# Chunked RWKV-7 recurrence rearranged: compact 32-wide diagonal blocks, the inverse of one chunk issued among the state and output of the chunk before

## What is computed

```python
def rwkv7_scan(r, w, k, v, a, b):
    def step(state, inp):
        r_t, w_t, k_t, v_t, a_t, b_t = inp
        sa = jnp.einsum("bhvk,bhk->bhv", state, a_t)
        state = (state * w_t[:, :, None, :] + sa[..., None] * b_t[:, :, None, :]
                 + v_t[..., None] * k_t[:, :, None, :])
        return state, jnp.einsum("bhvk,bhk->bhv", state, r_t)
...
def squared_relu_mlp(h, w_up, w_down):
    return jnp.square(jax.nn.relu(h @ w_up)) @ w_down
```

## Time and profile before

| | us |
|---|---|
| median of 3 runs (2734.05 to 2739.23) | 2734.75 |
| profiled execution | 2739.59 |
| its span, first to last instruction | 2737.8 |
| TensorE busy in it | 2587.3 (95%) |
| VectorE, ScalarE, GpSimd busy | 1136.0, 696.1, 320.1 |
| mean granted TensorE clock | 0.979 of 2.4 GHz |

### The profile page before, as it was taken

The page is one execution under the profiler, slowest core; times in us unless marked ns, Lnnn a source line. Parts: engine busy times, 40 slices in busy tenths (PEclk is TensorE's granted clock), DMA queues, the critical chain, the costliest instruction groups (busy, mean ns, idle before and its releaser), DMA issues.

```text
span 2737.8 us, 34644 instructions
## 1 busy us (share of the span) xinstructions
PE 2587.3 (95%) x13906; PEld 2140.4 (78%) x13906; DVE 1136.0 (41%) x1331; ACT 696.1 (25%) x1053; POOL 320.1 (12%) x242
## 2 busy tenths in 40 slices
PE   6999899898989999999999999977999999999998
PEld 5888688787887788888888878744778888888887
DVE  3344466666643333323333343277333332333332
ACT  4010134433321211211122122265231121112212
POOL 0000033332323200000000040043310000000000
PEclk8999999999989999999999999999999999999999
DMA  3221000000011111111111111100111111111112
GB/s 109 79 60 52 15 1 1 2 1 2 13 35 52 41 47 47 54 46 46 47 52 46 46 41 54 31 1 0 42 44 47 47 54 46 46 46 53 46 46 77
DMA packets 166311, 110.54 MB, mean 40 GB/s; under 512 B 3582, under 2 KB 163668, under 8 KB 166228
## 3 DMA queue, kind: packets, MB, share of 16 engines
q1 hardware_dynamic: 163756, 100.39, 12.3%
q0 software_dynamic: 2416, 8.91, 1.0%
q10 hardware_dynamic: 56, 0.01, 0.0%
HBM read 102.49 MB, written 6.29 MB: 40 GB/s over the span
## 4 chain that ended last, share of the span: by engine, by line
PE 83%; DVE 9%; ACT 4%; issue 3%; DVEq 0%; DMA 0%; POOL 0%; SPq 0%; ACTq 0%; POOLq 0%
PE ps L261 70%; PE ps L958 1%; PE ps L1368 1%; PE ps L961 1%; PE ps L947 1%; DVE probs L1396 1%; DVE softmax_stats L1401 1%; PE ps L913 1%; DVE mlp_lo L450 1%; DVE stage L447 1%; PE ps L975 1%; ACT stage L423 1%; PE ps L895 1%; ACT mlp_hi L425 1%; DVE x_level L1059 1%
## 5 line engine op out<-in xcount | busy, mean ns | idle before, releaser
L261 PE MATMUL ps<-h_hi,w_hi 128*128 128x512 f32 x1856 | 579.2, 393 | 23.3 <-DVE h_lo L1706 10.1
L261 PE MATMUL ps<-h_lo,w_hi 128*128 128x512 f32 x1856 | 575.6, 391 | 0.0
L261 PE MATMUL ps<-h_hi,w_lo 128*128 128x512 f32 x1856 | 574.3, 391 | 0.0
L222 ACT CAST w_hi<-w_raw 128x1024 fp32r<-128x1024 f32 x180 | 189.3, 1052 | 966.1 <-PE ps L261 966.1
L261 PEld LDWEIGHTS ps<-h_hi,w_hi 128*128 128x128 f32 x1856 | 347.8, 189 | 98.4 <-issue 14.8
L261 PEld LDWEIGHTS ps<-h_lo,w_hi 128*128 128x128 f32 x1856 | 350.8, 189 | 74.0
L261 PEld LDWEIGHTS ps<-h_hi,w_lo 128*128 128x128 f32 x1856 | 350.6, 189 | 73.8
L261 PE MATMUL ps<-mlp_hi,w_hi 128*128 128x512 f32 x1024 | 317.7, 391 | 10.7 <-DVE mlp_lo L450 10.7
L261 PE MATMUL ps<-mlp_lo,w_hi 128*128 128x512 f32 x1024 | 315.5, 389 | 0.0
L261 PE MATMUL ps<-mlp_hi,w_lo 128*128 128x512 f32 x1024 | 315.4, 389 | 0.0
L455 DVE TENSOR_TENSOR residual<-residual,ps 128x1024 f32<-128x1024 f32 x128 | 156.2, 1220 | 355.8 <-PE ps L261 355.8
(11 more groups left out here) (249 smaller groups left out, 2451.3 us busy)
## 6 DMA issues: line engine op xcount, KB each, us to landing
w_raw<-in_mlp_up SPq DMA_DIRECT2D x64, 512.0 KB, 4.0
w_raw<-in_mlp_down SPq DMA_DIRECT2D x64, 512.0 KB, 3.4
w_raw<-in_w_in_ab SPq DMA_DIRECT2D x26, 512.0 KB, 3.9
w_raw<-in_w_qkv SPq DMA_DIRECT2D x10, 512.0 KB, 3.9
x_in_tile<-in_x POOLq DMA_DIRECT2D x8, 512.0 KB, 4.2
w_raw<-in_w_out_ab SPq DMA_DIRECT2D x8, 512.0 KB, 4.1
w_raw<-in_w_o SPq DMA_DIRECT2D x8, 512.0 KB, 3.9
out<-out_chunk SPq DMA_DIRECT2D x8, 512.0 KB, 3.2
```

Of the source, the lines that this page charges most:

```text
L222: nc.scalar.copy(WH[:, slot], WR[:, slot]).then_inc(w_hi, 1)
L261: m = nc.tensor.matmul(acc(a_slot, half), ww, xx[:, k, half * HALF:(half + 1) * HALF], start=first, stop=last)
```

## The change

The hand-written order is replaced by one body per engine, unrolled: `body(n)`, n = -1 to 8, issues the inverse of chunk n, the state and output of chunk n-1 and the prep of chunk n+1 in one list. At levels 0 to 3 only the four 32x32 diagonal blocks of each head are computed, in compact tiles of 128 x 8 x 32: a product set is 32 products of 32x32, four row groups and column groups in turn. The update is accumulated in a PSUM bank which a set with the identity has started; ScalarE copies the bank to the block inverse, and VectorE transposes it 32x32 by 32x32 (an instruction that the kernel before doesn't have). The row products are computed in four parts between the levels, with 128 instead of 256 moving columns; all use the same two banks. The masks of the levels shrink to 32 columns. z and the product of `w_t` with the state are summed in PSUM, the state is kept as 64x64 blocks, and the copies of `v_chunk`, `lora_chunk` and the decay mask go. The first two down products of an MLP group are interleaved over k.

```diff
+            def first_pair(g, after):
+                t.wait_ge(w_lo, u0 + 8 * g + 4 + 3)
+                t.wait_ge(acc_free[0], a0_ // 2 + 6 * g + 3)
+                for n, (m, k) in enumerate(((0, 0), (0, 1), (0, 2), (1, 0), (1, 1), (0, 3), (1, 2), (1, 3))):
+                    if n < 3 or k == 3:
+                        t.wait_ge(act_lo, 4 * NG * l + 4 * g + 2 + k)
...
+        def body_pe(t, n):
+            inv, state, prep = 0 <= n < NT, n > 0, n + 1 < NT
+            c, e = n - 1, n + 1
+            def diag_products(bank_n, left, right, start):
+                for h in range(8):
+                    for q in range(4):
+                        m = MM(block_bank(bank_n, 32)[quarter(q), h], left[quarter(q), h], right[quarter(q), h],
...
+            def level_y(k):
+                if k:
+                    inv_act.wait(t, n, f"i{k - 1}")
+                    inv_pool.wait(t, n, "x")
+                else:
+                    inv_dve.wait(t, n, "x0")
+                inv_pe.done(diag_products(B_Y, XLC[:, k], TIC, "each"), f"y{k}")
+            def level_dt(k):
+                inv_act.wait(t, n, f"y{k}")
+                if k:
+                    inv_dve.wait(t, n, f"tt{k - 1}")
+                inv_pe.done(diag_products(B_T, TTC, YLC, "none"), f"dt{k}")
+            def row_products(q, b):
+                if q == 0 and b == 0:
+                    if state:
+                        st_dve.wait(t, c, "s1_1" if c < NT - 1 else "u")
+                elif b == 0:
+                    inv_dve.wait(t, n, "m1")
+                else:
+                    inv_dve.wait(t, n, f"{'mn'[q]}0")
...
+                        MM(out_[:, 0], left, ABK[rows, s, 0, 2 * b + j], start=True, stop=True)
+                        m = MM(out_[:, 1], left, RDEC[rows, s, 2 * b + j], start=True, stop=True)
...
+            if inv:
+                diag_products(B_T, TTC, diag_const(C_I32), "first")
+            if prep:
+                ... (head sums n2)
+            if inv:
+                level_dt(0)
+            if state:
+                ... (output products, first part)
+            if inv:
+                level_y(1)
+            if state:
+                ... (output products, last part, then the state products s)
+            if inv:
+                level_dt(1)
+                level_y(2)
+                row_products(0, 0)
+                level_dt(2)
+            if state:
+                st_act.wait(t, c, "o")
+                out_pe.done(MM(bank(B_OUT), blk, part(c, 4), start=True, stop=True), "mean")
+            if inv:
+                level_y(3)
+                row_products(0, 1)
+            if prep:
+                prep_act.wait(t, e, "spread")
+                ... (transposes nt)
+            if inv:
+                level_dt(3)
+                row_products(1, 0)
...
+        def body_dve(dve, n):
...
+            if inv:
+                block_transpose(3)
+                masked_products(0, 1, "m1")
+                masked_products(1, 0, "n0")
...
+                inv_pe.wait(dve, n, "dtt4")
+                W.done(nc.vector.tensor_copy(TIT[q0, :, q1], block_bank(B_T, 32)[q0, 0:8]), "tt4_0")
+                W.done(nc.vector.tensor_copy(TIT[q2, :, q3], block_bank(B_T, 32)[q2, 0:8]), "tt4_1")
+                masked_products(1, 1, "n1")
...
+            if state:
+                out_pool.wait(dve, c, "m2")
+                prep_pool.wait(dve, c, "lb")
+                out_dve.done(TT(part(c, 4), part(c, 4), BON[:, c % 2], ALU.add), "m4")
+                out_pe.wait(dve, c, "gate")
+                out_dve.wait(dve, c, "m4")
+                out_dve.done(TT(part(c, 0), part(c, 4), bank(B_OUT), ALU.mult), "yb")
+            if prep:
+                prep_pe.wait(dve, e, "bon")
+                V.done(TT(BON[:, e % 2], bank(B_PREP), part(e, 8), ALU.mult), "bon")
```

More of the change, by code:

```diff
@@ L576, in hybrid_trunk @@
         prep_dve = Track("prep_dve", ["kkr", "zws", "zas", "scan", "mid", "end", "d", "dx", "ka", "k2", "max", "rcp",
[L577 to L590, removed]
+                                      "kkn", "a_dec", "b0", "b_dec", "k_dec", "r_dec", "bon"])
+        inv_pe = Track("inverse_pe", ["diag", "y0", "dt0", "y1", "dt1", "y2", "p1_0", "dt2", "y3", "p1_1", "dt3", "p2_0",
+                                      "y4", "p2_1", "dt4", "dtt4", "tok0", "tok1", "y5", "tok2", "tok3", "dtt5", "nv"])
+        inv_act = Track("inverse_act", ["y0", "i0", "y1", "i1", "y2", "i2", "y3", "i3", "half", "y4", "tok0",
+                                        "tok1", "y5", "tok2", "tok3", "nv"])
+        inv_dve = Track("inverse_dve", ["mtc", "i", "tt", "ti", "x0", "tt0", "tt1", "tt2", "m0", "tt3", "m1", "n0", "t4", "tt4_0",
+                                        "tt4_1", "n1", "tt5"])
+        inv_pool = Track("inverse_pool", ["x"] + [f"full{q}" for q in range(4)])
+        st_pe = Track("state_pe", ["wt", "u", "o", "s"])
+        st_act = Track("state_act", ["wt", "o"])
+        st_dve = Track("state_dve", ["u", "gg", "s1_0", "s1_1", "s2_0", "s2_1"])
         out_pe = Track("out_pe", ["mean", "var", "vt", "gate"])
@@ L594, in hybrid_trunk @@
         out_pool = Track("out_pool", ["m2"])
[L595 to L608, removed]
@@ L623, in spread_back, with part, quarter, half_rows @@
[L623 to L627, removed]
+        def part(c, first):
+            return RKV[:, first:first + 4, c * P:c * P + P]
+        def quarter(i):
+            return slice(32 * i, 32 * i + 32)
+        def half_rows(i):
+            return slice(RH * i, RH * i + RH)
+        def block_bank(n, w):
+            return PS[:, n, :].rearrange("p (h m) -> p h m", m=w)
+        def by_parity(ap):
+            return ap.rearrange("p (j g) m -> p g j m", g=2)
@@ L629, in by_head, with diag_const @@
+        def diag_const(col, heads=8):
+            return over(CON[:, col:col + 32], heads)
         def by_head(ap, cols):
             return (ap.rearrange("p a (g m) -> p (a g) m", m=RH), cols.unsqueeze(2).to_broadcast([P, 2 * NP_, RH]))
[L634 to L659, removed]
@@ L684, in prep_pe_step @@
                 prep_dve.wait(t, e, "kkn")
                 prep_pool.wait(t, e, "rk2")
-                prep_pe.done(nc.tensor.matmul(bank(7), blk, T7[:, :], start=True, stop=True), "bon")
-        def prep_act_step(act, e, s, place):
-            A = nc.scalar.activation
-            if place == HEAD[0]:
+                prep_pe.done(MM(bank(B_PREP), blk, T7[:, :], start=True, stop=True), "bon")
+            if inv:
+                to_tokens(2)
+                to_tokens(3)
+                inv_act.wait(t, n, "y5")
+                inv_dve.wait(t, n, "tt4_1")
+                inv_pool.wait(t, n, "full3")
+                for h in range(8):
+                    m = MM(block_bank(B_T, RH)[top, h], Y5[low, h], TIT[low, h, low], start=True, stop=True)
+                inv_pe.done(m, "dtt5")
@@ new lines, in body_pe @@
+            if state:
+                out_dve.wait(t, c, "m1")
+                for p in range(4):
+                    m = MM(bank(B_OUT)[:, p], LOR[:, 2, p * P:(p + 1) * P], GL[:, c * P:c * P + P],
+                           start=True, stop=True)
+                out_pe.done(m, "gate")
+            if inv:
+                inv_dve.wait(t, n, "n1")
+                inv_act.wait(t, n, "tok3")
+                for h in range(8):
+                    m = MM(PS[:, B_M[0], RH * h:RH * h + RH], NTRK[:, h, 0], TOK[:, 3, RH * h:RH * h + RH],
+                           start=True, stop=True)
+                inv_pe.done(m, "nv")
@@ L702, in prep_act_step @@
+            if state:
+                st_pe.wait(act, c, "o")
+                waited(act, "act")
+                st_act.done(nc.scalar.copy(part(c, 4), bank(B_OUT)), "o")
+            if inv:
+                level_y(2)
+            if prep:
                 prep_act.wait(act, e, "e1")
                 prep_act.done(A(T3[:, :], T3[:, :], ACT.Exp, scale=KAPPA), "e2")
-            if place == 1:
                 prep_act.done(A(T4[:, :], T4[:, :], ACT.Exp, scale=-KAPPA), "e1x")
+            if inv:
+                block_copy(2)
@@ L706, in prep_act_step @@
+            if prep:
                 prep_pe.wait(act, e, "n2")
-                prep_act.done(A(NR[:, :], PS[:, 7, 0:2 * NP_], ACT.Sqrt), "nrm")
-            if place == "root":
+                prep_act.done(A(NR[:, :], PS[:, B_PREP, 0:2 * NP_], ACT.Sqrt), "nrm")
+            if state:
+                out_dve.wait(act, c, "d")
+                out_act.done(A(SQO[:, :], part(c, 4), ACT.Square), "sq")
+            if n == NT:
+                mixed_act(act, 0)
+                mixed_act(act, 1)
@@ L711, in prep_act_step @@
                 prep_act.done(nc.scalar.copy(dst, src), "spread")
-        def prep_dve_step(dve, e, s, place):
-            V, TT, STT = prep_dve, nc.vector.tensor_tensor, nc.vector.scalar_tensor_tensor
-            k = part(e, 4)
-            if place == HEAD[0]:
-                if not is_first(e):
```

(44 more changed lines are left out.)

776 lines of the change are left out of this document (342 added, 434 removed).

## The result

The changed kernel takes 2699.8 us (median of four, 2696.7 to 2702.1) against 2736.4 for the kernel before, measured beside it: ratio 0.9865, 95% interval 0.9848 to 0.9882. It is faster by 1.35%, and the forecast was slower, 2860. Its profiled execution took 2702.1, its span is 2700.3.

A forecast was written before the change was run, and what follows sets the result against it. TensorE was taken as the bound (95% busy). Bodies of 53.8 plus 22.8 us for low clock, 77, make the recurrence 643 for 503.7 (+139); with the MLP +128, so 2860 us, range 2675 to 2900.

The forecast's parts named there:

- The price of a set: Level products: 32 products of 32x32, 64 records at 25.5 ns issue, 1.65 us at full clock, 3.3 at half.
- The bound of 0.45: Lower bound for a set of 32x32 products, in us, if four places in turn share the time; upper bound 2.05.
- from dt3 to vt: Stretch of 10 us with the 2.5 us wait, var and small blocks, where TensorE's clock was expected to fall.
- tokens: Token products, y5 and bon, until the clock is back: low clock adds 3.8 us a body.
- dt0 and y2: Clock falls in stretches without wide products, 4.5 us to dt0, 4.1 from dt1 through y2; y2's wait for i1 0.75.
- m1: Wait of row_products(1, 0) on VectorE's mask m1, behind block_transpose(3) and i3: 2.5 us a body.
- nt: Wait of the nt transposes on ScalarE's spread, behind nrm's table load and VectorE's work: 1.3 us a body.
- n1: Wait of to_tokens(0) on mask n1, behind VectorE's copies after dtt4: 1.85 us a body.
- bon: Wait of the next body's zw on bon, behind six VectorE operations after dtt5: 1.7 us a body.
- The MLP: Interleaved down products remove 16 waits on mlp_lo: 10.7 us less, at worst 8.
- Sets at a quarter: Rival: sets cost a quarter of the price with the clock up, bodies of 47 us, 2640 us; chance 0.06.
- the clock stays: Rival: TensorE keeps full clock, bodies of 53.8 us, 2683 us in all, range 2660 to 2710; chance 0.25.

The follow-up runs named there:

- one_place: The changed kernel with each set's eight products of one 32x32 quarter run one after another, four places in sequence instead of in turn: 2848.9 us, ratio 1.0391.
- two_places: The changed kernel with each set taking its four places two at a time, quarters 0 and 1 in turn, then 2 and 3: 2737.5 us, ratio 0.9985.
- m1_first: The changed kernel with VectorE's mask m1 done before the transpose of block set 3: 2655.3 us, ratio 0.9673.
- moved2: The changed kernel with steps reordered in the engines' queues (masks m1, n1, bon chain, w_t copy, spread, y3 copy, dt1, GpSimd's masks): 2593.4 us, ratio 0.9454.
- filler_small: The changed kernel plus 48 unread 32x32 products inside each of four waits of every body: 2706.2 us, ratio 0.9880.
- moved3: moved2 with ScalarE's copy of the blocks i1 ahead of the two exponentials: 2582.8 us, ratio 0.9425.

## Why the prediction was wrong

**The price of a set failed, and with it the sum.** "That is issue, 25.5 ns a record. A set of 32 products is 64 records: 1.65." Measured: 0.56 from first to last start and 0.69 to the next product at full clock, 1.01 at half. The groups in the earlier trace rows had 16 records in one place. The forecast took their pace for TensorE's issue and carried it to four places in turn; one_place and two_places show that it belongs to the place. Ten sets at 0.69 instead of 1.65 are 9.6 us a body. The bound of 0.45 was in the text, and the forecast chose the far end because the groups' pace looked like a floor. The trace of before held a warning: loads of two row halves start together within one row, so places do overlap.

The rule of the Trainium skill cited for it (TensorE: Matmul & The Clock Gate, Wait — 56ns, not 53.3ns?), that start-to-start never drops below about 25 ns, does not hold for places in turn: 8.9 ns here. The other one (TensorEngine Tiling (Array Packing), Theoretical Speedup), up to 4x, came near: 3.1 with four places at full clock.

**The clock fell where forecast, at less than half the price.** The steps "from dt3 to vt" and "tokens" hold in every middle body (20.5 us low, once 23.9); of the places dt0 and y2 one or the other is low for 3.4 or 6.8 us. Predicted: +22.8 a body. Measured: 54.7 less 45.2 = 9.5. The same mis-sized term is in it: the price at half clock took 3.3 a set, and the forecast let the low clock last because long sets kept the wide work away. one_place, in which that term is nearly true (1.84 a set at full clock, 2.99 at half), has bodies of 74.7 (forecast 77), a recurrence of 628 (643) and 2849 in all (2860, ratio 1.039). Its clock costs 21.7 a body by the same estimate (work 35.9 and ten sets dearer by 1.15, waits 5.6) against 22.8 forecast. So the sum was about right for that kernel.

**The rest of the body's work was right.** The other products came to 45.7 less 16.5 for the sets, 29.2. Measured: 35.9 of work less ten sets of 0.69, 29.0.

**The waits were right in sum, off in parts.** 8.1 forecast, 9.3 measured: m1 2.06 (2.5), nt 1.07 (1.3), n1 1.17 (1.85), bon 1.15 (1.7), y2 1.38 (0.75). Two were not priced: u on `w_t` 0.98, for ScalarE's copy stands behind the square of the keys, which waits for VectorE; and y0 on x0 0.76.

**The MLP** gave 11.5 (10.7 forecast). The spilled rows cost nothing, as forecast: no wait on their read shows. Body 8 took 26.9 (26), the prologue 21.5 (20.7), body 7 49.9 and body 0 50.0 (72 and 62, by the term above).

**The rivals.** None had the pair that came true, a set at 0.69 and the clock down for 24 us a body. "Sets at a quarter" had the nearer price (0.45 a set), with a chance of 0.06, and joined it to a clock that stays up. The two unknowns were priced apart but not crossed: with the lower bound of the set, the low clock costs little and the kernel is faster whether or not it falls. 2699.8 lies within the range of 2675 to 2900, and within the 2660 to 2710 of "the clock stays", whose price of a set and whose clock were both wrong: two errors that cancel, not a hit.

Summed by body: the six full bodies took 329.4 where 462 was forecast, 133 less; body 7 22 less, body 0 12 less, prologue and body 8 2 more: 165, which is what the recurrence came out under the forecast (478.3 against 643). Of the 22 us of a full body 9.6 are the set's price at full clock and some 13 the clock's.

## What to carry to other kernels

Price a small product by the place it goes to: the pace of one place is no floor for several in turn, so order small blocks with the place as the innermost loop (149 us of 2700 here). Where TensorE's stretches are made of small or thin products, look at the granted clock and expect a wait in a low stretch to cost more than its length: here twice and more (m1_first and moved), but only its own size once the clock was mostly up (moved2). One swapped pair of lines was worth 44 us. When two unknown prices meet in a sum, work out all four corners before choosing the likeliest.

## What the runs showed of the hardware

An addition or product of VectorE with two operands from SBUF that starts while a GpSimd product runs ends only after it. The rows are from the timeline of the changed kernel: two operations of VectorE of one size. The first started just before GpSimd's product and kept its usual 0.43; the second started while that ran.

```profile
507.27 0.43 DVE L1000 TENSOR_TENSOR diag_inv_t<-diag_mt,constants 128x256 f32<-128x256 f32 x1
507.73 1.91 DVE L1002 TENSOR_TENSOR diag_inv_t<-diag_inv_t,constants 128x256 f32<-128x256 f32 x1
```

```profile
507.32 2.05 POOL L1118 TENSOR_TENSOR diag_x<-diag_mt,constants 128x768 f32<-128x768 f32 x1 [1.33 <-DVE diag_mt L997]
```

The second ended at 509.64, GpSimd's at 509.37, and y0's wait of 0.74 (on x0, behind it) follows. It took 1.91 in all eight bodies, each time ending 0.28 after GpSimd's. In moved2, with GpSimd's work later, it took 0.43, and the delay moved to a later operation of VectorE (2.30 instead of 0.68 for 512 columns, ending 0.55 after GpSimd's), which nobody waited for so soon. The Trainium skill (GPSIMD Engine Reference, 1. Specifications) says the two engines share SBUF interfaces and contend where VectorE has two SBUF inputs; the trace agrees. The transpose of 128x256 by blocks of 32 took 0.45, the lower of the two bounds.

Long rows of small records bring pauses: in filler_small, where up to 224 stand in a row at 9 ns each, TensorE stood for up to 2.7 us in the middle of products that wait for nothing. In moved3, where nothing holds y2 back after dt1 and the state products, such pauses are the largest idle time left (8.5 us in 12, the longest 1.6). That the instructions come too late is the likely reading; no run tests it.
